# Differential attention: the order and the row shape of the score and mask products

## The reference, cut to what matters

```python
for qb in range(seq_len // Q_BLOCK):            # 4 blocks of 128 queries
    q0, kend = qb * Q_BLOCK, (qb + 1) * Q_BLOCK
    s = jnp.einsum("bqhcd,bkhcd->bhcqk", q[:, q0:kend], k[:, :kend])
    chunk_end = (q_idx // CHUNK + 1) * CHUNK    # CHUNK = 64
    mask = jnp.arange(kend)[None, :] < chunk_end[:, None]
    p = jax.nn.softmax(jnp.where(mask, s, -jnp.inf), axis=-1)
    attn = p[:, :, 0] - lam * p[:, :, 1]
    outs.append(jnp.einsum("bhqk,bkhe->bqhe", attn, v[:, :kend]))
```

## Time and profile before

| | |
|---|---|
| median of 3 runs | 1427.07 us (1424.55 to 1427.35) |
| profiled execution, time | 1429.59 us |
| profiled execution, span | 1427.8 us |
| mean granted TensorE clock | 0.929 |
| PE busy | 1285.5 us, 90% of the span |
| DVE busy | 858.2 us, 60% |
| ACT busy | 497.9 us, 35% |
| POOL busy | 430.6 us, 30% |
| score products (L1935) | 128 passes, from 782.4 to 987.2 us |
| mask products (L1938) | 128 passes, from 782.8 to 987.9 us |

### The profile page before, as it was taken

How to read it: one execution, slowest core, us unless ns; L and a number is a source line. 1 busy time by engine, 2 the same in 40 slices (tenths; PEclk the granted TensorE clock), 3 DMA queues, 4 the chain that set the end, 5 groups by cost and what they waited for, 6 DMA issues and landing times.

```text
span 1427.8 us, 17491 instructions
## 1 busy us (share of the span) xinstructions
PE 1285.5 (90%) x6312; PEld 1019.1 (71%) x6312; DVE 858.2 (60%) x1107; ACT 497.9 (35%) x749; POOL 430.6 (30%) x273
## 2 busy tenths in 40 slices
PE   5532699979999999999999999988999999999995
PEld 1322588868888888888777667665778888888884
DVE  8999868648988644324683565764674444443223
ACT  2143233214433334223431344433534334432311
POOL 3992011125454433200012423320024443341001
PEclk9765799959999999999999999978999999999997
DMA  8002988703766422323223212111103232223311
GB/s 332 1 1 37 160 262 336 266 1 148 277 252 246 166 89 88 118 89 118 70 81 112 59 45 89 44 45 59 59 30 118 88 106 100 88 90 116 103 75 59
DMA packets 35431, 164.97 MB, mean 116 GB/s; under 512 B 4529, under 2 KB 14001, under 8 KB 17201
## 3 DMA queue, kind: packets, MB, share of 16 engines
q1 hardware_dynamic: 34368, 163.97, 34.3%
q10 hardware_dynamic: 1008, 0.27, 0.1%
HBM read 156.95 MB, written 3.08 MB: 112 GB/s over the span
## 4 chain that ended last, share of the span: by engine, by line
PE 77%; DVE 15%; issue 3%; DMA 2%; SPq 1%; ACT 1%; POOL 1%; DVEq 0%; ACTq 0%; POOLq 0%
PE psum L1736 16%; PE psum L1737 16%; PE psum L1738 16%; PE psum L1877 5%; PE psum L1879 5%; PE psum L1878 5%; PE psum L1935 3%; PE psum L1938 2%; PE psum L1620 1%; PE psum L1959 1%; PE psum L1821 1%; SPq L375 1%; PE psum L1920 1%; PE psum L1922 1%; PE psum L1921 1%
## 5 line engine op out<-in xcount | busy, mean ns | idle before, releaser
L1736 PE MATMUL psum<-hhi,whi 128*128 128x512 f32 x960 | 384.6, 401 | 4.5 <-DVE hlo L1307 2.7
L1737 PE MATMUL psum<-hlo,whi 128*128 128x512 f32 x960 | 378.8, 395 | 0.0
L1738 PE MATMUL psum<-hhi,wlo 128*128 128x512 f32 x960 | 378.7, 395 | 0.0
L1185 DVE TENSOR_TENSOR wlo<-raw,whi 128x2048 fp32r<-128x2048 f32 x82 | 198.0, 2415 | 171.1 <-ACT whi L691 171.1
L691 ACT ACTIVATE whi<-raw 128x2048 fp32r<-128x2048 f32 x81 | 155.1, 1915 | 176.8 <-PE psum L1879 146.1
L567 POOL TENSOR_TENSOR ca<-ca,cb 128x512 f32<-128x512 f32 x44 | 143.2, 3254 | 242.7 <-ACT ca L801 242.7
L1736 PEld LDWEIGHTS psum<-hhi,whi 128*128 128x128 f32 x960 | 183.3, 191 | 46.2 <-issue 6.1
L1738 PEld LDWEIGHTS psum<-hhi,wlo 128*128 128x128 f32 x960 | 183.2, 191 | 39.4
L1737 PEld LDWEIGHTS psum<-hlo,whi 128*128 128x128 f32 x960 | 183.3, 191 | 36.5
L1401 DVE SCALAR_TENSOR_TENSOR ca<-psum,convp,ca 128x511 f32<-128x511 f32 x44 | 32.9, 749 | 201.2 <-ACT ca L797 201.2
L1877 PE MATMUL psum<-ghi,whi 128*128 128x512 f32 x352 | 137.2, 390 | 1.5 <-DVE wlo L1185 1.5
(11 more groups left out here) (344 smaller groups left out, 1804.6 us busy)
## 6 DMA issues: line engine op xcount, KB each, us to landing
raw<-in_units SPq DMA_DIRECT2D x92, 1024.0 KB, 4.8
ada_ring<-in_ada_w SPq DMA_DIRECT2D x40, 1024.0 KB, 4.8
ada_raw<-in_ada_w SPq DMA_DIRECT2D x8, 1024.0 KB, 14.8
toep<-toeplitz_rows SPq DMA_DIRECT2D x32, 128.0 KB, 9.5
qk_sw<-ca SPq DMA_DIRECT2D x32, 128.0 KB, 2.3
u<-in_x_blocks SPq DMA_DIRECT2D x1, 2048.0 KB, 14.0
x<-in_x_t SPq DMA_DIRECT2D x1, 2048.0 KB, 9.4
out_t<-x SPq DMA_DIRECT2D x8, 256.0 KB, 2.0
```

Of the source, the lines that this page charges most:

```text
L1185: TT(wlo[:, s, :], raw[:, s, :], whi[:, s, :].bitcast(F32), ALU.subtract).then_inc(split_lo, 1)
L1736: M(out, w_hi, hi[:, k, :], start=(k == 0), stop=False)
L1737: M(out, w_hi, lo[:, k, :], start=False, stop=False)
L1738: return M(out, w_lo, hi[:, k, :], start=False, stop=(k == KT - 1))
```

## The change

Both score products of a step are issued first, component 0 and then component 1, and the two mask products follow. A mask product no longer has one row: it has the 64 rows of its component's half, of which the first row holds what the single row held before (and -1e30 for the first 64 queries), and the 63 others hold zero. So the mask tile takes all partitions instead of one, POOL clears it whole, waits for its own clearing, and writes two rows, 0 and 64. PE waits for four increments of mask_ready instead of three. Nothing else is changed; the number of instructions on PE is the same.

```diff
-        maskw = at("maskw", [1, 2, P], F32, o); o += 2 * P * 4
+        maskw = at("maskw", [P, 2, P], F32, o); o += 2 * P * 4
...
-            nc.gpsimd.memset(maskw[0:1, 0, 0:HD], MASKED).then_inc(mask_ready, 1)
-            nc.gpsimd.memset(maskw[0:1, 0, HD:P], 0.0).then_inc(mask_ready, 1)
-            nc.gpsimd.memset(maskw[0:1, 1, :], 1.0).then_inc(mask_ready, 1)
+            nc.gpsimd.memset(maskw[:, 1, :], 1.0).then_inc(mask_ready, 1)
+            nc.gpsimd.memset(maskw[:, 0, :], 0.0).then_inc(mask_ready, 1)
+            pool.wait_ge(mask_ready, 2)
+            for c in range(2):
+                nc.gpsimd.memset(maskw[HD * c:HD * c + 1, 0, 0:HD], MASKED).then_inc(mask_ready, 1)
...
-            pe.wait_ge(mask_ready, 3)
+            pe.wait_ge(mask_ready, 4)
...
                     M(psum[:, 4 + c, 0:width], qk[rows, s, 0, P * qt:P * qt + P], qk[rows, s, 1, 0:width],
                       start=True, stop=True)
-
-                    ins = M(psum[:, 4 + c, width - HD:width], maskw[0:1, 0, :], maskw[0:1, 1, 0:HD],
+                for c in range(2):
+                    rows = slice(HD * c, HD * c + HD)
+                    ins = M(psum[:, 4 + c, width - HD:width], maskw[rows, 0, :], maskw[rows, 1, 0:HD],
                             start=False, stop=True, skip_group_check=True)
                 ins.then_inc(s_psum, 1)
```

## The result

The changed kernel takes 1387.97 us (median of 4 runs, 1383.9 to 1391.37), against 1425.81 for the kernel before in the same comparison: a ratio of 0.9737, 95% interval 0.9704 to 0.977. That is 38 us, 2.6%; forecast were 1394.5 and 32.6.

The account below looks back on a forecast made before the run. PE was taken to set the pace. Steps 0 and 3 (20.7) plus steps 1 and 2 (13.6) less the clock (1.7) gave 32.6 us off the median of 1427.07, so 1394.5, range 1384 to 1412.

Parts of the forecast that it names:

- The halves overlap: Attention scores on PE: both array halves run at once, saving 5.17 us a head, 41.4 over eight heads.
- The overhead of 0.20 for each change of shape: Score steps on PE: unhidden weight load and array emptying cost 0.20 us per change, four changes or 0.8 a step.
- What PE keeps: Attention heads: steps 0 and 3 keep all, 20.7 us; steps 1 and 2, partly held by DVE beside POOL, keep 13.6.
- The clock: PE in the attention: one further 3.4 us stretch at the low level, charged as a loss of 1.7 us.
- POOL's mask: Mask set-up on POOL ahead of the attention: four memsets and a wait, hidden; without cover some 0.6 us.
- One pass apart: Rival, scores on PE: second half starts when the first begins its second pass; 1400 us, chance 0.10.
- No overlap: Rival, scores on PE: halves take turns, only changes of shape saved, 15.9 us; 1411 us, chance 0.12.
- no effect: Rival, scores on PE: changing row half empties the array as changes of shape do; 1427 us, chance 0.06.
- slower: Rival, all heads: longer waits of PE drop the clock and outweigh the saving; 1431 us, chance 0.04.
- DVE and POOL falling out well: Rival, heads 2 to 6: DVE meets POOL's gap, keeping 6.8 us more, with less low clock; 1384 us, chance 0.10.

Follow-up runs that it names:

- the late rope: Changed kernel, but from head 4 of the pipeline on POOL starts rope only after DVE has written step 1's attention; 1395.42 us, ratio 0.9781.
- narrow rope: Changed kernel with POOL's rope over 64 columns instead of 512 beside attention heads 2 to 6, leaving out most positions; 1374.5 us, ratio 0.9631.
- shape-only kernel: Changed kernel with its 64-row masks but the old order: score 0, mask 0, score 1, mask 1; 1389.25 us, ratio 0.9738.

## Why the prediction was right, and where it was off

*The halves overlap.* Right, and this was the open point. Steps were forecast at 0.58, 0.79, 1.00 and 1.21 us; steps 0, 2 and 3 are 0.59, 1.02 and 1.22 in the rows above, and step 1 is 0.80 in every head. The S5 products were the right rows to go by, though their halves have different output partitions: the same partitions in two banks do as well.

*The overhead of 0.20 for each change of shape.* Right for the changed step. Two components in one step cost one unhidden load and emptying; the masks' work proper is 0.16, as left of the 0.36. That a change of shape drains the array agrees with the Trainium skill (TensorEngine Tiling (Array Packing), section Tiling Modes): with one-row masks in the new order, the one more change and the masks in turn cost 0.42 us a step. No run here parts such a drain from the load that nothing hides. The prediction put it down to a mask product of another shape between the scores that no overlap was to be seen before. Of that, only the shape counts: with 64 rows the mask may stand between them.

*What PE keeps.* Right in kind, and too high. In heads 4 and 5 step 1's attention is written 8.0 and 7.9 us after its scores start, 1.21 and 1.23 less than before, for a forecast of one POOL instruction, 1.25. Head 1 passed the norm in POOL's gap, as forecast (4.0 us instead of 8.9). Head 3 is a miss: its write, 7.1 us after the scores start (869.51), was to stay with POOL and comes 7.9 us after them. Before, POOL waited 0.41 us for the swap there, and the small instructions of the norm passed in 0.17 each; in head 3 of the changed kernel POOL has no such wait, and they take 1.22 and 1.19.

```profile
848.01 2.51 POOL L602 TENSOR_TENSOR qk_sw<-qk_sw,sinb 128x512 f32<-128x512 f32 x2
```

The heads that ran at full clock on both sides, 1, 2 and 4, fell by 4.60, 2.72 and 3.74 us, 11.1 together; forecast were 5.17, 3.51 and 3.83, 12.5. The missing 1.4 is DVE again. The row maximum of step 2 starts 2.2 to 2.8 us after the end of its scores in heads 2 to 5 (1.5 at most before), and that of step 3 in heads 1 and 2 starts 1.3 and 0.8 us after it (0.1 before). In head 1 `weigh` of step 2 now waits 1.04 us; before, `weigh` of step 1 waited there, 0.43. So the chains that I had called free in step 3 are so only while DVE is. For all heads there is an estimate: half of the difference at the low clock (30.7 and 6.8 us in the attention) taken off its 40.6 us leaves 28.6 that PE kept, where the forecast has 32.7 for the same stretch.

The prediction also counted head 6 with 4 and 5. It is another case: its filler is part of the output projection and has five portions instead of eight, and in the kernel before PE waited there for 1.93 and 2.34 us:

```profile
953.83 0.71 PE L1959 MATMUL psum<-v_sb,att_t 128*128 128x128 f32 x4 [1.93 <-ACT att_t L882]
...
961.99 1.65 PE L1959 MATMUL psum<-v_sb,att_t 128*128 128x128 f32 x6 [2.34 <-ACT att_t L882]
```

*The clock.* This term had the wrong sign. I charged 1.7 us for one more stretch at the low level. In the two profiles the attention with the 10 us behind it had 30.7 us at 0.50 before and 6.8 after; head 5, 28.4 us before, is 21.7 now, a gain of 6.7 where 3.8 was forecast without the clock. By the mean granted clock of all executions (0.927 over 46 of the kernel before, 0.931 over 10 of the changed one) the low level held for 208 and 191 us of the span (twice the missing share, by the span), 17 less. Across the executions of the kernel before, a microsecond more at the low level goes with 0.34 more in time, so the clock gave some 6 us instead of taking 1.7. This is an estimate from a correlation; by the two profiles alone it would be 12. The difference to the charge, 7.5 us and more, exceeds the 5.2 by which the forecast of 32.6 fell short of 37.8; the rest is what PE kept less. Two terms were off in opposite directions, and that the sum came out so near is in part luck.

Why the clock rose is settled only in part. With slow scores and no waits the low level stays (27 us of it), with fast scores and waits made longer (the late rope) 17 us come back, with fast scores and none of these waits (narrow rope) there is none. Each of these is one profiled execution. They suggest that both count, and that the scores with four changes of shape counted for more than I gave them; what brings the low level is not shown.

*POOL's mask.* Hidden, as forecast: its last instruction ends at 724.3, long before the first scores at 779.1.

*The rivals.* One pass apart: no, the first passes begin within 0.03 us. No overlap, no effect, slower: no. (The slower rival's arithmetic was off: 69 us more at the low level, on 31, would be about half of the heads' length and not two thirds.) DVE and POOL falling out well: partly in head 6 (5.2 us instead of 9.0), not in heads 2 to 5.

## What to carry to other kernels

Make neighbouring small products one shape, even if most rows of one are zeros: a mask of 64 rows costs 0.16 us for both components, while a single row between them cost four loads and emptyings, and kept two halves of the array from running side by side. Put the saving against the chain that takes over: in the three heads at full clock the scores got 15.5 us shorter and the heads 11.1, the rest went into waits for DVE, and the next gain was in cutting POOL's instructions short, since DVE waits for their ends. The clock was the term with the wrong sign here: when the products of a stretch get denser, it can give as well as take, and the forecast should have carried both. And where two halves run on their own, the last product in the program need not be the last to end. Here the last mask product alone raises s_psum, with masks of equal width in both halves; no run tests unequal ones.

## What the runs showed of the hardware that I had not expected

The row halves of the array take their products independently of the order in the program: in the shape-only kernel score 1 starts within 0.03 us of score 0, ahead of mask 0, which stands before it. That DVE waits for POOL was in the prediction; new is how closely it follows. A small DVE instruction on 4 elements a row takes 0.17 us alone and until the end of the running POOL instruction otherwise: 1.2, 0.6 to 0.7 and 0.4 us beside POOL instructions that follow one another every 1.25, 0.69 and 0.42. TENSOR_TENSOR and SCALAR_TENSOR_TENSOR instructions wait so too (1.24 and 1.19 in the late-rope kernel), not only TENSOR_SCALAR; RECIPROCAL on 2 elements (0.17 us with and without POOL beside it), the row maxima from PSUM (0.69 for step 1) and the sum over SBUF that begins the norm (0.68) showed no such wait.
